# A two-layer streaming encoder step: the feed-forward products as one pass over each half of the frames

## The reference

```python
for layer in range(2):
    xp, xs = rms_norm(hp, g[0]), rms_norm(hs, g[0])
    # layer 0: gated MLP beside sliding-window attention, then one output projection
    # layer 1: trailing mean pooling over 4 channel groups, then c_w per group
    m = mixer(xp, xs)
    hp, hs = hp + rms_norm(mp, g[1]), hs + rms_norm(ms, g[1])
    hp = hp + rms_norm(swiglu(rms_norm(hp, g[2]), w_in, w_out), g[3])   # hs likewise

def swiglu(h, w_in, w_out):          # w_in 1024 x 5632, w_out 2816 x 1024
    gu = h @ w_in
    return (silu(gu[..., :D_FF]) * gu[..., D_FF:]) @ w_out
```

## Time and profile before

| | us |
|---|---|
| three timed runs | 1101.49, 1097.10, 1100.05 |
| median | 1100.05 |
| profiled execution, its own time | 1097.38 |
| its span, first to last instruction | 1095.1 |
| PE busy | 1059.6 (97%) |
| DVE busy | 507.5 (46%) |
| ACT busy | 363.1 (33%) |
| DMA, mean over the span | 82 GB/s |

### The profile page before, as it was taken

How to read it: one execution, slowest core, us unless ns; L and a number is a source line. 1 busy time by engine, 2 the same in 40 slices (tenths; PEclk the granted TensorE clock), 3 DMA queues, 4 the chain that set the end, 5 groups by cost and what they waited for, 6 DMA issues and landing times.

```text
span 1095.1 us, 19945 instructions
## 1 busy us (share of the span) xinstructions
PE 1059.6 (97%) x8219; PEld 1029.8 (94%) x8219; DVE 507.5 (46%) x817; ACT 363.1 (33%) x598; POOL 43.7 (4%) x48
## 2 busy tenths in 40 slices
PE   6999999989999999999999899899999999999997
PEld 4799789989999999999999898899999999999995
DVE  4387752854444444342222769544434444322225
ACT  5522354542222222222222675322222222222222
POOL 0070220000000000000000011000000000000000
PEclk9999999999999999999999999999999999999998
DMA  6422122123233223223223210232332232223212
GB/s 223 97 64 81 39 59 67 50 72 101 77 92 92 84 77 96 86 75 97 88 82 92 66 44 20 78 96 77 96 96 77 84 92 83 85 87 93 78 52 82
DMA packets 166532, 89.69 MB, mean 82 GB/s; under 512 B 11976, under 2 KB 163647, under 8 KB 166492
## 3 DMA queue, kind: packets, MB, share of 16 engines
q1 hardware_dynamic: 164620, 86.99, 27.0%
q10 hardware_dynamic: 1648, 1.78, 0.5%
q0 software_dynamic: 224, 0.35, 0.1%
HBM read 86.53 MB, written 2.58 MB: 81 GB/s over the span
## 4 chain that ended last, share of the span: by engine, by line
PE 84%; DVE 10%; ACT 3%; issue 3%; DMA 1%; SPq 0%; POOL 0%; ACTq 0%; DVEq 0%
PE ps L454 27%; PE ps L456 26%; PE ps L455 26%; DVE h L1591 2%; DVE tmp L1561 1%; DVE wlo L1315 1%; DVE acc_pre L1577 1%; PE ps L519 1%; DMA x_tok<-in_x_sample_dram 1%; DVE xlo L1565 1%; ACT whi L939 1%; PE ps L864 1%; PE ps L918 1%; PE ps L472 0%; DVE va L1374 0%
## 5 line engine op out<-in xcount | busy, mean ns | idle before, releaser
L454 PE MATMUL ps<-xhi,whi 128*128 128x256 f32 (+1 forms) x1600 | 466.2, 291 | 9.7 <-DVE xlo L1565 5.8
L455 PE MATMUL ps<-xlo,whi 128*128 128x256 f32 (+1 forms) x1600 | 461.9, 289 | 0.0
L456 PE MATMUL ps<-xhi,wlo 128*128 128x256 f32 (+1 forms) x1600 | 460.8, 288 | 0.0
L1315 DVE TENSOR_TENSOR wlo<-raw,whi 128x1024 fp32r<-128x1024 f32 (+2 forms) x175 | 196.7, 1124 | 269.4 <-ACT whi L939 265.2
L454 PEld LDWEIGHTS ps<-xhi,whi 128*128 128x128 f32 x1600 | 303.1, 189 | 14.7 <-DVE xlo L1565 8.5
L455 PEld LDWEIGHTS ps<-xlo,whi 128*128 128x128 f32 x1600 | 303.5, 190 | 0.0
L456 PEld LDWEIGHTS ps<-xhi,wlo 128*128 128x128 f32 x1600 | 303.3, 190 | 0.0
L939 ACT ACTIVATE whi<-raw 128x1024 fp32r<-128x1024 f32 (+2 forms) x176 | 168.0, 954 | 196.2 <-PE ps L456 171.7
L456 PE MATMUL ps<-mhi,wlo 128*128 128x256 f32 (+1 forms) x704 | 203.5, 289 | 0.0
L454 PE MATMUL ps<-mhi,whi 128*128 128x256 f32 (+1 forms) x704 | 202.5, 288 | 0.0
L455 PE MATMUL ps<-mlo,whi 128*128 128x256 f32 (+1 forms) x704 | 202.4, 288 | 0.0
(11 more groups left out here) (195 smaller groups left out, 811.3 us busy)
## 6 DMA issues: line engine op xcount, KB each, us to landing
raw<-in_ffn_w_in_dram SPq DMA_DIRECT2D x88, 512.0 KB, 3.8
raw<-in_ffn_w_out_dram SPq DMA_DIRECT2D x32, 384.0 KB, 3.1
raw<-in_ffn_w_out_dram SPq DMA_DIRECT2D x32, 320.0 KB, 2.9
raw<-in_ab_w_in_dram SPq DMA_DIRECT2D x10, 512.0 KB, 3.9
x_tok<-in_x_prompt_dram SPq DMA_DIRECT2D x4, 512.0 KB, 5.4
raw<-in_ab_w_in_dram SPq DMA_DIRECT2D x8, 256.0 KB, 3.5
raw<-in_ab_w_out_dram SPq DMA_DIRECT2D x8, 256.0 KB, 2.9
raw<-in_ab_w_out_dram SPq DMA_DIRECT2D x16, 128.0 KB, 3.2
```

What stands on the lines that cost most here:

```text
L454: pe.matmul(out, wh, xh, start=first, stop=False)
L455: pe.matmul(out, wh, xl, start=False, stop=False)
L456: return pe.matmul(out, wl, xh, start=False, stop=last)
L1315: dve.tensor_tensor(wlo[:, s, 0:n], raw[:, m % NRAW, 0:n], whi[:, s, 0:n].bitcast(F32), ALU.subtract)\
```

## The change

The units of the feed-forward part are no longer used for both halves in turn. For each layer there are four passes: gate and up for half 0, gate and up for half 1, output for half 0, output for half 1. Each pass loads and splits all its units again. `mhi` and `mlo` become separate buffers for the halves. One list `UNITS` gives the order of all units in the program, and everything is written out, without hardware loops; `NRAW` becomes 3. The norms and the pooling of one half are cut into steps that hang on unit numbers (slots) of a pass of the other half: the table `STAGE` says behind which unit PE makes a sum or a spread, and at which unit ACT and DVE do their steps, there ahead of that unit's split. Residual and squares go in pairs of blocks. The second norm is now applied to the input (`x_scale`), so that gate and up need no scaling. Where ACT keeps the Silu table, the root is made on POOL with a power. Pooling turns `h` with plain transposes and takes the norm in when the rows are kept; the frames of each half are now a pair of bands with a carry of 16 columns. In the output projection of layer 0, blocks 2 and 3 of the second half get units of their own (two more loads), and the six blocks 4 to 7, 2 and 3 of the second half stand last.

```diff
-U_C = U_FO[0] + 4 * KC
-NRAW, NSPLIT = 2, 4
+C_AFTER = ((15, 16), (19, 21))
+STAGE = {
+    (0, 1): {"sum": 1, "spread": 2, "scale": (3, 5, 7, 9), "fold": 10, "pre": 12, "again": 13, "x": (14, 16, 18, 20)},
+    (1, 0): {"sum": 0, "spread": 1, "scale": (1, 2, 3, 4), "fold": 6, "pre": 8, "rows": (7, 7, 8, 8),
+             "keep": (9, 9, 10, 10), "bands": (11, 11, 12, 12, 13, 13, 14, 14)},
+    (2, 0): {"sum": 20, "spread": 21, "scale": (21, 22, 23, 24), "fold": 26, "pre": 28, "again": 29,
+             "x": (29, 30, 31, 32)},
...
+    (3, 0): {"sum": 1, "spread": 2, "scale": (2, 4, 6, 8), "rows": (10, 10, 11, 11)},
+}
+NRAW, NSPLIT = 3, 4
...
+OUT_DEPTHS = (*range(KC), 2, 3)
+OUT_STEPS = [(0, None), (1, None)] + [(u, 0) for u in range(2, KC)] + [(u, 1) for u in range(4, KC + 2)]
...
+            def ffn_out(layer, b, run):
...
+                for slot, m in enumerate(FO_PASS[layer, b]):
...
+                    sl = m % NSPLIT
+                    for c in range(first, last):
+                        w = slice((c - first) * P, (c - first + 1) * P)
+                        mm = product(flat(2 * b + d % 2, 0, n), whi[:, sl, w], wlo[:, sl, w],
+                                     mhi[b][:, c, :], mlo[b][:, c, :], c == 0, c == FC - 1)
+                    mm.then_inc(w_used, 1)
+                    run(slot)
...
+            ffn_in(0, 0, stepper(norms(0, 1)))
+            ffn_in(0, 1, idle)
+            ffn_out(0, 0, idle)
+            ffn_out(0, 1, stepper(pooling(0)))
+            ffn_in(1, 0, stepper(pooling(1)))
+            ffn_in(1, 1, idle)
+            ffn_out(1, 0, idle)
+            ffn_out(1, 1, stepper(last_half()))
```

The same calls stand in ACT's and DVE's programs. DVE's steps of a chain, and its order at a unit:

```diff
+                    if j == 3:
+                        add_z(2 * layer + 1, b, d)
+                    run(slot)
+                    if m + 4 < len(UNITS):
+                        lo_part(m + 4)
...
+            def residual_pair(s, b, p):
...
+                dve.tensor_tensor(tmp[:, :, c], src, pair_of(r_post, b), ALU.mult).then_inc(z_scaled[b], 1)
+                if p >= 2 and s < 3:
+                    add_square(s, b, p - 1)
+                dve.wait_ge(z_scaled[b], 4 * s + p + 1)
+                dve.tensor_tensor(h[:, 2 * p:2 * p + 2, c], h[:, 2 * p:2 * p + 2, c], tmp[:, :, c], ALU.add)\
+                    .then_inc(h_added[b], 1)
```

More of the change, by code:

```diff
@@ L53 @@
 NT = len(TILES)
[L56 to L63, removed]
 PIECES = ((0, 6), (6, 12), (12, 17), (17, 22))
-MIXER_STORES = (5, 7)
+STORES_AB, STORES_POOL = 5, 7
 U_STEPS = (3, 3, 2, 3, 3, 2, 3, 3, 2, 4, 4)
@@ L122, in unit_dmas, with stepper, run @@
         return 2
-    return 3 if U_OUT <= m < U_FI[0] else 1
+    return 3 if UNITS[m][0] == "out" else 1
 def loaded(m):
     return 16 * sum(unit_dmas(j) for j in range(m % NRAW, m + 1, NRAW))
+def stepper(chain):
+    due = [next(chain, None)]
+    def run(slot):
+        while due[0] is not None and due[0] <= slot:
+            due[0] = next(chain, None)
+    return run
+LAST = 1 << 20
 def shape_constants():
@@ new lines, in norms, with pooling @@
+            def norms(s, b):
+                at = STAGE[s, b]
+                yield at["sum"]
+                sum_squares(s, b, 0)
+                yield at["spread"]
+                spread(s, b, 0)
+                if s == 3:
+                    return
+                yield at["pre"]
+                sum_squares(s, b, 1)
+                if s == 1:
+                    return
+                yield at["again"]
+                spread(s, b, 1)
+            def pooling(b):
+                yield from norms(1, b)
+                for i, slot in enumerate(STAGE[1, b]["rows"]):
+                    yield slot
+                    turn_rows(b, i)
+                for i, slot in enumerate(STAGE[1, b]["bands"]):
+                    yield slot
+                    band(b, i)
+                yield from norms(2, b)
@@ L1134, in after_mixer_ab @@
+                bank = OUT_BANKS[e]
+                if b == 0 and u >= 4:
+                    act.wait_ge(out_half_done, u - 3)
+                else:
+                    act.wait_ge(w_used, U_OUT + u + 1)
+                d = OUT_DEPTHS[u]
+                for half in (0, 1) if b is None else (b,):
+                    evacuate_z(0, half, out_order(e), z[:, d, frames(half)], part(bank, half), gain(0, 1, d))
             def after_mixer_ab():
[L1136 to L1138 removed]
@@ new lines, in _ @@
+            ffn_in(0, 1, idle)
+            warm(ACT.Sqrt)
+            ffn_out(0, 0, idle)
+            ffn_out(0, 1, stepper(pooling(0)))
+            warm(ACT.Silu)
+            ffn_in(1, 0, stepper(pooling(1)))
+            ffn_in(1, 1, idle)
+            warm(ACT.Sqrt)
+            ffn_out(1, 0, idle)
+            ffn_out(1, 1, stepper(last_half()))
+            root(3, 1, 0)
+            keep_spread(3, 1, 0)
+            for i in range(6):
+                if i not in TAIL_DVE:
+                    t, half = TAIL_ORDER[i]
+                    keep_y(1, i, t, half, i % 6)
@@ new lines, in pooling @@
+            def pooling(b):
+                yield from norms(1, b, b)
+                for i, slot in enumerate(STAGE[1, b]["bands"]):
+                    yield slot
+                    band_low(b, i)
+                yield from norms(2, b, b)
+            idle = lambda slot: None
+            ffn_in(0, 0, stepper(norms(0, 1, 1)))
+            ffn_in(0, 1, idle)
+            ffn_out(0, 0, idle)
+            ffn_out(0, 1, stepper(pooling(0)))
+            ffn_in(1, 0, stepper(pooling(1)))
+            ffn_in(1, 1, idle)
```

1439 lines of the change are left out of this document (754 added, 685 removed).

## The result

The changed kernel takes 1087.3 us (median of 4 runs, 1083.9 to 1087.6), the kernel before 1100.3 in the same comparison. The ratio is 0.9889, 95% interval 0.9864 to 0.9914: 1.1% faster, where 1060 us (3.6%) was forecast, and 1084 was the upper end of the range that counts the first two rivals in. The profiled execution took 1087.63 us with a span of 1085.3.

What follows compares the result with a forecast made beforehand. Bound by PE's product stream, with a DVE and ACT chain around it: 150 + 849 + 29.5 + 1 + 5 + 3 = 1037.5 us, tail 17, span 1054.5, 1057 profiled, median 1060; range 1050 to 1068.

Steps and rivals of the forecast that it cites:

- the first two rivals: Loads bounding the output passes (chance 0.12) and chain steps delaying splits (0.13); with both, the range reaches 1084 us.
- the allowance for chains inside passes: Passes carrying the other half's chain: DVE some 4 us late where 6 are allowed; 3 us allowed for all.
- Rival 2: Feed-forward passes: chain steps ahead of splits make PE wait, 16 us at eight stages; 1072 to 1080 us; chance 0.13.
- Power on POOL: Spreads: nearest row 1.04 us against 2.6 us left; at 5 us each, five spreads would lose 12 us.
- Product time: From 150 us to the last product: 6786 matmuls at 0.125 us, 849 us, unchanged by the change.
- The seam: Between output projection and first pass: PE waits 2 to 3 us, then 2 more; 5 us taken.
- Sums, spreads, turning and bands: PE's work between products, with no filling ahead of the last product: 29.5 us in place of 76.
- The tail: Behind the last product: 17 us instead of 20.1, the residual of half 0 having left it.
- Loads: Feed-forward weights loaded twice, 69 MB more: hidden, with 512 KB landing in 3.8 us and three buffers.
- rival 1: Output passes: landings grow and loads bound them, if short pieces exceed 3.9 us; 1074 to 1097 us; chance 0.12.
- rival 3: All passes: DMA engines can't hold the rate; below a sustained 165 GB/s (45 us more) the kernel gets slower; chance 0.07.
- a third buffer alone gains nothing where PE never waits now: Weight loads: a third raw buffer by itself wins no time while PE never waits.

Runs made afterwards that it cites:

- experiment 2: Changed kernel with only ACT's chain step moved behind its hi split, DVE's pair still ahead of its lo split: 1066.9 us, ratio 0.9720.
- experiment 5: Changed kernel with ACT's step behind its split and spreads one unit later (1064.2 us), now without feed-forward weight loads for the second half's passes: 1064.8 us.
- experiment 1: Changed kernel with the chain step moved behind the weight split on both ACT and DVE in the feed-forward passes: 1103.1 us, ratio 1.0045.

## Why the prediction was wrong

The median is 27.3 us above the forecast, the profiled execution 30.6 above the 1057 forecast for one (I had put the median 2.7 us above it, and it is 0.3 below). By the table above, waits are 14.8 us of that, product time 14.3, sums, bands and turning 1.6.

**The step that failed** is the allowance for chains inside passes: "So PE should just not feel it. I allow 3 us for all these places together." I had summed DVE's own instructions, a pair ahead of a split, and found it 4 us late where 6 are allowed. In experiment 2 DVE has just that work in that order, and PE never waits for `wlo`: DVE's own work was no trouble, as the sum had it. What it left out is that ACT's square stood ahead of ACT's `hi` split, and so hung the `lo` split on the pair by way of the other engine. Rival 2 had this as a condition ("if each step waits for its partner on ACT or POOL") at 16 us; the ring cost 20 us (1087.3 to 1066.9), 13.1 of it as waits for `wlo`. I gave it 0.13, and had read nothing for or against it in the order of the instructions, where it stood to be read.

**Power on POOL.** Rival 2 bounded it by 1.04 us and 5 us; it took 0.86 to 1.89 us. With the ring opened PE still waited 1.6 us for it, at two spreads.

**Product time.** 849 us was mis-sized. With the ring opened it is 861.9 us for 6819 matmuls, 0.1264 us each and not 0.125: I had taken the mean of the best stretch, while separate passes run at 118.1 and 133.3 ns in gate and up and 120.0 and 132.2 in the output. That is 10 us, all at full clock. The paces of the passes together make 0.1258 us a matmul, which is 6 of the 10; the other 4 are 44 single matmuls behind sums, spreads and bands, where the distance to the next is 0.19 to 0.24 us. Part of this was there already: by the same count the kernel before took 859.0 us for 6809 matmuls where my term was 852, 3.5 of it in two stretches at the lower clock (222 to 227 and 686 to 691 us). So some 4 of the 10 us stood in the trace that I had read, and some 6 came with the passes. The kernel after has 4.4 us more, most of it at the lower clock. Behind the wait of 2.81 us that ended at 632.04 us the granted clock fell:

```profile
632.00:636.00 4.00, 3.96 (x20) 3.99 (x21) 3.61 (x7) 3.37 (x6) 0.00 (x0) 0.57 0.48 133
636.00:640.00 4.00, 4.00 (x37) 4.00 (x35) 1.08 (x1) 2.49 (x4) 0.00 (x0) 1.00 0.68 187
```

0.57 is mostly the lower level, 1.2 GHz: 15 matmuls stood 0.213 us apart in place of 0.119, 1.4 us. A stretch of the same size followed the bands of the running stream's frames at 697 us (the granted clock was 0.50 from 697 to 700.3), where PE had not waited.

**What held.** The seam, with 5 us in the forecast, had 1.5 us at the sum, 1.0 at `xlo` and 0.9 at the next spread. Sums, spreads, turning and bands: 31.1 against 29.5. The tail: 17.0 against 17. Loads: landings of 3.9 us for 512 KB where I had 3.8, and of 3.1 and 3.5 for the short pieces where rival 1 needed more than 3.9. Rival 1 falls by these; rival 3 by the 176 to 180 GB/s held from 200 to 331 and 473 to 535 us, where it had 165, and for half 1 both fall by experiment 5. By the Trainium skill, "DMA: Bandwidth & Descriptors", section "Latency and other measured facts", the latency of HBM is 0.2 us on average and 2 us at high load. With the engines busy for 0.62 of the time the trace shows 0.1 to 0.4 us more for a landing, and not the 1.8 that I had estimated from the two figures; no run here shows a higher load held for long. The sentence "a third buffer alone gains nothing where PE never waits now" was about the kernel before; with the passes the third buffer carries 88 us, more than I had thought.

With ACT's step moved the kernel measures 1064 to 1067 us, inside the forecast's own range of 1050 to 1068: the gain from covering the seams was there, and 20 of some 33 us were given back by the place of ACT's step. That it lies there owes something to luck: product time was 10 us over its term, and waits, with 6.0 us, 3 under theirs.

## What to carry to other kernels

When two engines work on two streams in turn, draw the order on both engines as one ring: count which instruction waits for which across them, not each engine's sum of work. If in both the step of stream one stands ahead of stream two's, or in both behind it, each unit costs the sum of the steps on both engines (3.7 us in the changed kernel and 4.2 in experiment 1, against 2.2 in experiment 2); put it ahead on the engine that starts stream one and behind on the one that starts stream two. Doubled loads cost nothing here at 0.62 of the DMA engines' time with three buffers, and 88 us went with the third buffer, so that count is worth testing by itself. Steps hung on unit numbers need the numbers checked against the profile whenever the order around them moves.

## What the hardware showed besides

- A power of 128 x 3 on POOL took 0.86 to 1.89 us, one of 32 x 1 took 0.55.
- The same matmul of 256 columns went at 118.5 ns or 120.0 as its moving operand's tiles lay 1040 or 1024 bytes apart; of 288 columns at 132.2 or 133.5 ns (waits taken out) when the whole operand lay 704 bytes further on.
- A 2.81 us wait of PE was followed by about 3.3 us at the lower clock; waits of 1.92 us (to 753.34 us) and 2.49 us (to 762.57) were not. In experiment 1 a wait of 1.66 us (to 653.55 us) was: the granted clock was 0.62 from 654 to 658 us. So the length of one wait didn't decide it in these traces.
